# Two-layer attention and state-space block on one core: loads reordered, key weights' halves in further buffers, gate taken by halves of its PSUM pair

## What is computed

```python
for l in range(2):
    sh, sc, gt = split(silu(c) @ w_ada[l] + b_ada[l])          # the same with c_ctx for the context
    h  = rms_norm(x, norm_pre[l]) * (1 + sc) + sh
    hc = rms_norm(ctx, norm_pre[l]) * (1 + scc) + shc
    if l == 0:  # qa, ka, va, ga, qb, kb, vb, gb = split(h @ w_in); two kinds of attention, 16 heads, 4 key groups
        y, yc = attn_mixer(...)                                 # softmax attention, times silu(gate), @ w_out
    else:       # z, xbc, dt = split(h @ w_in); conv, silu; a chunked two-way state-space scan in 8 groups
        y = gated_rms_norm(scan + D * x, z, norm_w) @ w_out     # y * silu(z), normed by group
    x = x + gt * rms_norm(y, norm_post[l])
```

## Time and profile before

| what | value |
|---|---|
| median of 3 runs | 1668.16 us (1666.35 to 1669.1) |
| the profiled execution, own time | 1661.65 us |
| its span (first to last instruction) | 1659.9 us |
| PE busy | 1449.7 us, 87% of the span |
| PEld busy | 1270.8 us, 77% |
| DVE busy | 994.7 us, 60% |
| ACT busy | 703.4 us, 42% |
| POOL busy | 303.2 us, 18% |
| mean granted PE clock | 0.942 of full speed |
| transfers | 124.41 MB, 75 GB/s over the span |

### The profile page before, as it was taken

How to read it: one execution, slowest core, us unless ns; L and a number is a source line. 1 busy time by engine, 2 the same in 40 slices (tenths; PEclk the granted TensorE clock), 3 DMA queues, 4 the chain that set the end, 5 groups by cost and what they waited for, 6 DMA issues and landing times.

```text
span 1659.9 us, 23265 instructions
## 1 busy us (share of the span) xinstructions
PE 1449.7 (87%) x8440; PEld 1270.8 (77%) x8440; DVE 994.7 (60%) x1782; ACT 703.4 (42%) x1456; POOL 303.2 (18%) x294
## 2 busy tenths in 40 slices
PE   5789899999989889869995899899898989897797
PEld 5678787888778788758874787888788887886575
DVE  5575666667657676644206566767676767666322
ACT  5221344434334433323216455555545555555331
POOL 0000000000000000002223241414233231413143
PEclk9999899999999999979997999999999999996799
DMA  9243111211112111124411111111101111110431
GB/s 357 72 144 127 39 49 57 87 47 47 57 38 88 54 48 48 48 95 146 158 45 63 54 52 39 63 38 51 62 28 62 38 63 38 57 70 0 171 134 64
DMA packets 37957, 124.41 MB, mean 75 GB/s; under 512 B 5392, under 2 KB 5648, under 8 KB 37904
## 3 DMA queue, kind: packets, MB, share of 16 engines
q1 hardware_dynamic: 33296, 113.21, 19.5%
q10 hardware_dynamic: 4608, 10.49, 2.0%
HBM read 109.00 MB, written 14.68 MB: 75 GB/s over the span
## 4 chain that ended last, share of the span: by engine, by line
PE 50%; DVE 17%; issue 13%; ACT 9%; POOL 8%; DMA 3%; SPq 0%; DVEq 0%; ACTq 0%; POOLq 0%
PE psL L1763 12%; PE psL L2062 4%; PE psC L1763 4%; POOL xw L1726 3%; PE psS L1748 3%; PE psS L1750 3%; PE psS L1749 3%; PE psV L1748 3%; PE psV L1750 2%; PE psV L1749 2%; POOL Hlo L1732 2%; PE psL L1748 2%; DVE smax L1216 2%; PE psL L1750 2%; DVE PTlo L1255 2%
## 5 line engine op out<-in xcount | busy, mean ns | idle before, releaser
L1763 PE MATMUL psL<-hhi,whi 128*128 128x512 f32 x320 | 132.7, 415 | 0.0
L1763 PE MATMUL psL<-hlo,whi 128*128 128x512 f32 x320 | 131.5, 411 | 0.0
L1763 PE MATMUL psL<-hhi,wlo 128*128 128x512 f32 x320 | 130.6, 408 | 0.0
L1611 POOL TENSOR_TENSOR rq<-vq,half 128x6 f32<-128x6 f32 x10 | 16.1, 1606 | 601.3 <-DVE vq L1109 601.3
L1615 POOL TENSOR_TENSOR wlo<-wraw,whi 128x1024 fp32r<-128x1024 f32 x34 | 81.6, 2399 | 236.2 <-ACT whi L570 140.1
L1748 PE MATMUL psV<-PThi,Vhi 128*128 128x256 f32 (+1 forms) x224 | 71.5, 319 | 38.2 <-DVE PTlo L1255 27.6
L1763 PE MATMUL psC<-hhi,whi 128*128 128x256 f32 x296 | 88.9, 300 | 17.4 <-DVE wlo L1075 7.4
L2062 PE MATMUL psL<-h1hi,whi 128*128 128x512 f32 x256 | 103.2, 403 | 0.0
L2062 PE MATMUL psL<-h1hi,wlo 128*128 128x512 f32 x256 | 101.6, 397 | 0.0
L2062 PE MATMUL psL<-h1lo,whi 128*128 128x512 f32 x256 | 101.4, 396 | 0.0
L1255 DVE TENSOR_TENSOR PTlo<-psT,PThi 128x256 fp32r<-128x256 f32 (+3 forms) x96 | 67.9, 707 | 42.1 <-ACT PThi L711 41.9
(11 more groups left out here) (399 smaller groups left out, 4722.9 us busy)
## 6 DMA issues: line engine op xcount, KB each, us to landing
wraw<-in_w_ssm SPq DMA_DIRECT2D x48, 512.0 KB, 3.2
wraw<-in_w_in SPq DMA_DIRECT2D x40, 512.0 KB, 4.5
wraw<-in_w_out SPq DMA_DIRECT2D x32, 512.0 KB, 4.0
ada<-in_w_ada SPq DMA_DIRECT2D x16, 512.0 KB, 15.1
wraw<-in_w_ada_late SPq DMA_DIRECT2D x16, 512.0 KB, 5.3
X<-in_xc SPq DMA_DIRECT2D x12, 512.0 KB, 8.7
y_spill<-Yst SPq DMA_DIRECT2D x16, 384.0 KB, 2.6
X<-y_spill ACTq DMA_DIRECT2D x16, 384.0 KB, 3.2
```

Source lines behind the costliest of these rows:

```text
L1763: last = PE_.matmul(out, a, b, start=i == 0 and not shared, stop=i == 3 * KT - 1, skip_group_check=True)
```

## The change

It has four edits, three on the first 175 us and one in the state-space groups. Edits without an effect on any order (names of semaphores, three signals instead of two for a group's z) are left out of the diff.

1. SP issues `early_load(0)` to `(2)`, three token tiles, `early_load(3)`, the other three token tiles, then `early_load(4)` and on. The three tables `costab`, `sintab`, `rowt` are loaded right behind the third tile of `w_in`, before the wait for `s_h_lo`; their buffers and `PThi`, `PTlo` move to the end of the allocation, and `junk0` is gone: the tanh of `crow` lies in the last two `ada` tiles until they are loaded (`early_load(7)` now waits for its use), the reductions' unused products in free parts of `hhi` and `hlo`.
2. Kind 0 of odd tiles 1 and 3 has its halves in `PThi` and `PTlo`, buffers of the attention that are free in this stage. So the halves of kind 0 are made one tile earlier: w = 2 within tile 0's stage, w = 2g+4 in group g behind `gate_tile(4g)`. `made(w)` gives the count that w has in the new order. SP's waits for raw buffers follow it.
3. `key_hi` and `key_lo` of groups 0 and 1 come ahead of `Vhi` and `Vlo`, with semaphores of their own (`s_key_hi`, `s_key_lo`). `q_hi(4)` and `q_lo(4)` come right behind the first head's evacuation and rope.
4. In the state-space groups z's second half-product is made for blocks 2 and 3 first, then 0 and 1; tanh and `sz` are made in two instructions of 512 columns, the second bank first. `cb(0)` waits for the first of these, the steps for the second. `gsel` is copied ahead of `GP`, with one semaphore for both.

```diff
     with ExitStack() as s:
...
-        junk0 = sbuf(s, "junk0", [P, 2, D_MODEL])
+    tanh_rows = ada[:, ADA_EARLY - 2:ADA_EARLY].rearrange("p n a b -> p n (a b)")
+    sum_junk = [h[:].rearrange("p k t -> p (k t)")[:, 6 * TOK:6 * TOK + D_MODEL] for h in (hhi, hlo)]
...
+    def made(w):
+
+        if 3 <= w < W_HEAD0 + 1:
+            return w + 2 if w % 2 else w
+        return w + 1
+
+    def weight_buffers(e, kind):
+
+        if kind == 0 and isinstance(e, int) and e < GROUPS and e % 2:
+            return tuple(b[:].rearrange("p t q -> p (t q)")[:, 0:D_MODEL].rearrange("p (a b) -> p a b", a=KT) for b in (PThi, PTlo))
+        return whi[:, kind], wlo[:, kind]
...
-        early_load(0)
-        early_load(1)
-        for t in range(TT):
+        def x_load(t):
+
             sp.dma_start(X0[:, t, :], io["xc"][t]).then_inc(s_x_loaded[t // 2], 16)
 
+        for k in range(3):
+            early_load(k)
+        for t in range(TT // 2):
+            x_load(t)
+        early_load(3)
+        for t in range(TT // 2, TT):
+            x_load(t)
+
...
-        for k in range(2, KT):
+        for k in range(4, KT):
+            if k == KT - 1:
+                sp.wait_ge(s_silu_rows, 2)
             early_load(k)
             if k == KT - 3:
                 w_in_load(0)
                 w_in_load(1)
         w_in_load(2)
-        w_in_load(3)
-        for u in range(NR, NR + 2):
-            sp.wait_ge(s_weight_lo, u - 3)
-            w_in_load(u)
-        sp.wait_ge(s_h_lo, KT)
         sp.dma_start(costab[:], io["cos"]).then_inc(s_tables_loaded, 16)
         sp.dma_start(sintab[:], io["sin"]).then_inc(s_tables_loaded, 16)
         sp.dma_start(rowt[:], io["rows"][ROWS["sink"][0]:ROWS["sink"][1]].partition_broadcast(P)).then_inc(s_tables_loaded, 16)
+        w_in_load(3)
+        for u in range(NR, NR + 2):
+            sp.wait_ge(s_weight_lo, made(u - NR))
+            w_in_load(u)
+        sp.wait_ge(s_h_lo, KT)
...
         h_scaled(0)
         h_scaled(1)
+        weight_hi(1, 0, 2, 1)
...
             q_lat(g, norm, scale)
-            weight_hi(g + 1, 0, (2 * g + 2) % NR, (2 * g + 2) // NR + 1)
+            if g + 2 <= GROUPS:
+                weight_hi(g + 2, 0, (2 * g + 4) % NR, (2 * g + 4) // NR + 1)
...
+            if g < 2:
+                key_hi(g)
             act.wait_ge(s_v_transposed, g + 1)
...
-            if g < 2:
-                key_hi(g)
         q_ctx(GROUPS, False, 1.0)
         q_lat(GROUPS, False, 1.0)
+        q_hi(GROUPS, 0)
         gate_ctx(GROUPS)
         gate_lat(GROUPS)
         key_hi(3)
-        q_hi(GROUPS, 0)
...
-            act.wait_ge(s_z_weight_used, 2 * g + 2)
-            A_.activation(thz[:], psS[:, :], ACT.Tanh, scale=0.5).then_inc(s_z_tanh, 1)
+            for n in range(2):
+                x = slice(512 * (1 - n), 512 * (2 - n))
+                act.wait_ge(s_z_weight_used, 3 * g + 2 + n)
+                A_.activation(thz[:, x], psS[:, x], ACT.Tanh, scale=0.5).then_inc(s_z_tanh, 1)
...
         for k in range(2, KT):
             h_split(k)
+            if k == 3:
+                weight_lo(2, 0, 2)
...
             rope(g)
-            weight_lo(2 * g + 2, 0, (2 * g + 2) % NR)
             gate_tile(4 * g)
+            if g + 2 <= GROUPS:
+                weight_lo(2 * g + 4, 0, (2 * g + 4) % NR)
             gate_tile(4 * g + 1)
...
         rope(GROUPS)
+        q_lo(GROUPS, 0)
         key_normed(3)
         gate(GROUPS, 0, 0)
         gate(GROUPS, 0, 1)
         key_lo(3)
-        q_lo(GROUPS, 0)
...
-            dve.wait_ge(s_z_tanh, g + 1)
-            V_.scalar_tensor_tensor(sz, thz[:], 1.0, psS[:, :], ALU.add, ALU.mult).then_inc(s_z_silu, 1)
+            for n in range(2):
+                x = slice(512 * (1 - n), 512 * (2 - n))
+                dve.wait_ge(s_z_tanh, 2 * g + n + 1)
+                V_.scalar_tensor_tensor(sz[:, x], thz[:, x], 1.0, psS[:, x], ALU.add, ALU.mult).then_inc(s_z_silu, 1)
...
-            z(1, (0, 1))
             z(1, (2, 3)).then_inc(s_z_weight_used, 1)
+            z(1, (0, 1)).then_inc(s_z_weight_used, 1)
             log_decays(0)
-            pe.wait_ge(s_z_silu, g + 1)
+            pe.wait_ge(s_z_silu, 2 * g + 1)
             pe.wait_ge(s_bc_lo, g + 1)
             cb(0)
+            pe.wait_ge(s_z_silu, 2 * g + 2)
```

More of the change, by code:

```diff
@@ L151, in build @@
         junkm = sbuf(s, "junkm", [P, 1, D_MODEL])
+        PThi = sbuf(s, "PThi", [P, TT, 2 * P], f32r)
+        PTlo = sbuf(s, "PTlo", [P, TT, 2 * P], f32r)
+        rowt = sbuf(s, "rowt", [P, 8])
+        nsink = sbuf(s, "nsink", [P, 8])
+        costab = sbuf(s, "costab", [P, SEQ])
+        sintab = sbuf(s, "sintab", [P, SEQ])
     ph.close()
@@ L252, in build @@
     s_rope_step = sem("rope_step")
-    s_q_hi, s_q_lo = sem("q_hi"), sem("q_lo")
+    s_q_hi, s_q_lo, s_key_hi, s_key_lo = sem("q_hi"), sem("q_lo"), sem("key_hi"), sem("key_lo")
     s_qk_square_sums, s_qk_variance, s_qk_rstd = sem("qk_square_sums"), sem("qk_variance"), sem("qk_rstd")
@@ L568, in weight_hi @@
             act.wait_ge(s_raw_weights_loaded[slot], 16 * use)
-            free_hi_lo(act, w, par, tile)
-            A_.activation(whi[:, par], wraw[:, slot], ACT.Copy).then_inc(s_weight_hi, 1)
+            if par == 0 and isinstance(tile, int) and 0 < tile <= GROUPS:
+                if tile > 1:
+                    act.wait_ge(s_q_lat_proj, tile - 1)
+            else:
+                free_hi_lo(act, w, par, tile)
+            A_.activation(weight_buffers(tile, par)[0], wraw[:, slot], ACT.Copy).then_inc(s_weight_hi, 1)
         act.wait_ge(s_small_loaded, 64)
         A_.activation(cth[:], csilu[:], ACT.Tanh, scale=0.5).then_inc(s_silu_c_step, 1)
-        A_.activation(junk0[:], crow[:], ACT.Tanh, scale=0.5).then_inc(s_silu_rows, 1)
+        A_.activation(tanh_rows, crow[:], ACT.Tanh, scale=0.5).then_inc(s_silu_rows, 1)
         for t in range(TT):
@@ L1072, in weight_lo @@
         def weight_lo(w, par, slot):
-            dve.wait_ge(s_weight_hi, w + 1)
-            V_.tensor_tensor(wlo[:, par], wraw[:, slot], f(whi[:, par]), ALU.subtract).then_inc(s_weight_lo, 1)
+            dve.wait_ge(s_weight_hi, made(w) if isinstance(w, int) else w + 1)
+            hi, lo = weight_buffers(w // 2 if isinstance(w, int) else w, par)
+            V_.tensor_tensor(lo, wraw[:, slot], f(hi), ALU.subtract).then_inc(s_weight_lo, 1)
         early_sums(0)
@@ L1155, in _ @@
                 key_lo(2)
+            if g < 2:
+                key_lo(g)
             if g >= 2:
@@ L1165, in _ @@
                 last.then_inc(s_k_rstd_diag, 1)
-            else:
-                key_lo(g)
             gate_tile(4 * g + 2)
@@ L1760, in project @@
                 k, m = divmod(i, 3)
-                a = (whi, whi, wlo)[m][:, par, k, :]
+                hi, lo = weight_buffers(e, kind)
+                a = (hi, hi, lo)[m][:, k, :]
                 b = (hhi, hlo, hhi)[m][:, k, toks]
```

59 lines of the change are left out of this document (27 added, 32 removed).

## The result

| | kernel before | changed kernel |
|---|---|---|
| median | 1668.63 us (4 runs, 1666.35 to 1672.08) | 1641.81 us (4 runs, 1639.39 to 1644.03) |
| profiled execution, own time | 1661.65 us | 1644.03 us |
| its span | 1659.9 us | 1642.3 us |
| PE, DVE, ACT, POOL busy | 1449.7, 994.7, 703.4, 303.2 us | 1445.0, 995.0, 704.0, 303.0 us |

The changed kernel is faster, by 1.6%: ratio 0.9837, 95% interval 0.9815 to 0.9859. The medians lie 26.8 us apart, the two profiled executions 17.6. Forecast were 1648.8 us and a difference of 19.4.

The account below looks back on a forecast made before the run. PE, busy 87% of the span, was taken as the bound, through standing still or lower clock. Terms -18.7 - 0.85 + 2.3 - 2.2 = -19.4 us, from median 1668.16 to 1648.8 us; range 1638 to 1657.

Parts of the forecast that it names:

- Edit 2, 18.7 us: Key and value stage: shorter waits and no slow tails at tiles 1 to 3, 7.62 + 5.08 + 5.98 us gained.
- All three gaps: PE's waits at kind 0 of three tiles in the key stage: 7.4, 3.33 and 6.7 us, plus slow matmuls behind.
- the margin at kind 1: Key stage: kind 1's low half ready at 83.7, wanted at 84.0; 0.3 us spare in group 0, 0.5 in group 1.
- Edit 3, 0.85: Before attention: one 0.95 us subtraction leaves DVE's stretch before `reduce_max`; gain 0.85 us, bounds 0 and 3.8.
- Edit 1, a loss of 2.3: First loads: last tokens land at 26.04 instead of 20.92, PE's first transposes move to 37.25; loss 2.3 us, bounds 0 and 5.1.
- Edit 4, "0.27 us a group, 2.2 for eight": State-space groups: `cb(0)` hides under the gate's second half, first step comes 0.27 us earlier; 2.2 us for eight, low bound 0.
- The clock rival: State-space groups: the shorter gap of some 2.3 us avoids the clock's fall; 14 us more, hence 1635; chance 0.12.
- Waits added, 0: Added waits in each group and for each attention head lie next to waits ending later; 0, bounds 0 and 1 us.
- The second wait: State-space groups: a short further wait of PE, after the wait of about 2.3 us on the silu.
- the forecast's own 1644 to 1654: Whole kernel: range in us of the main forecast without rivals, chance 0.63; with rivals 1638 to 1657.

Follow-up runs that it names:

- the trace with filling in its groups: Kernel before with 16 matmuls, their result overwritten, added where PE stood idle in seven state-space groups; 1658.70 us, ratio 0.9954.

## Why the prediction was right, and where it was off

**Edit 2, 18.7 us: right in place and nearly in size.** All three gaps went, bank `psC` was late next, the margin at kind 1 held (0.66 us where 0.3 was put). Up to tile 1 the sum said -6.13 + 2.3 = -3.83 and the traces show 77.49 - 80.92 = -3.43. From tile 1 to the norm it said 12.55; the traces show 89.81 - 78.70 = 11.1. The missing 1.4 is the row at 144.70: I took it that a gap of 1.3 us has nearly no slow tail, from a single row. Of the ten traces with the changed key stage eight have it at 4.4 to 4.6 us, with the granted clock falling at that row, and two at 3.08. The three traces with the old key stage have 3.06 to 3.09. So a gap of 1.3 us can have a tail; what decides is not settled. The tails of the old form are not fixed either: 4.34, 4.60 and 5.46 us in the trace before, 5.46 in all three of the trace with filling in its groups, which is most of why the norm is 14.5 us apart in one pair of traces and 17.6 in another. The forecast for edits 1 and 2, 16.4, lies between.

**Edit 3, 0.85: right,** 0.79 measured. **Edit 1, a loss of 2.3: right,** 2.3 to 2.9 measured; the 2.56 us per MB of the earlier trace rows carried it. The tokens' squares came at 26.38, where transfers in order put them at 26.04, so what the Trainium skill (DMA: Bandwidth & Descriptors, Queues, rings and completion order) says of transfers that complete out of order did not bear here. That this edit is a loss the experiment with the old order confirms in the trace; its median alone would not.

**Edit 4, "0.27 us a group, 2.2 for eight": this is the term that was mis-sized.** As a shortened path it was well put: the wait is 2.30 us as forecast, the first step comes 0.25 us earlier (0.27 forecast), and the edit is worth 0.18 a group once the clock is out of it. The Trainium skill (VectorE: DVE Perf Modes, The TRN2 errata) led to an estimate of 0.18 too, but by a cost of 0.16 for the split; the rows show 0.06, 1.27 against 1.21, so the agreement is not the page's. The mistake was to price the gap without what follows it, though edit 2 was priced with its tails. Over seven groups the edit is worth 7.1 us against the same kernel with the old gate, 4.2 against the kernel before (521.67 - 517.43), where the forecast has 1.9.

The clock rival asked whether the clock stays up behind the shorter gap (14 us). In the changed kernel it does not: it falls in all seven groups, for 3.4 us in six and nearly 7 in one. The price was also wrong. The clock kept up in all seven groups is worth 6.3 us to the kernel before, not 14: the group of 73.86 us, taken as still losing one stretch, loses nothing, as a group takes 73.83 to 73.86 with the clock up; PE then waits about 1 us for the update of the state instead. The rival drew on the Trainium skill (TensorE: Matmul & The Clock Gate, Part 1), by which a shorter gap is caught less often. The traces bear this out in part. Of 14 gaps of 2.83 us (the kernel before and the changed one with the old gate) none escapes and 11 have the long stretch; of 56 gaps of 2.30 us, in the eight traces with the halves and without filling, 2 escape and 13 have it.

The traces say more on the length. In all these 70 groups the stretch is the long one where the clock had fallen 0.27 us or more before PE went on (24 groups), and in the other 46 it is 3.4 us or there is none; there the clock fell 0.20 us before or later, or not at all. With the old gate it had fallen 0.55 us before in the group shown (1038.35 against 1038.90), and a group with the long stretch takes 75.13 to 75.19 us, while its falls follow each other at 75.09: the next gap meets the fall at nearly the same place, and the long stretch repeats. The kernel before is caught late three times, then early in the fourth group, and stays so for all that follow; the changed kernel with the old gate is caught early from the first on. With the halves such a group takes 74.65, the next gap comes 0.4 us earlier against the fall, and after one or two groups the long stretch ends. That is what the halves bought from the clock. Where the first group meets the fall differs from one execution to another.

**Waits added, 0: right within what can be seen.** The second wait that the forecast had shows as 0.4 us from the last matmul of `cb(0)` to the first step, instead of 0.12; no other new wait of PE stands in the groups.

**The sum against the two measures.** From the traces: 14.5 up to the norm, 0.8 in front of attention, 4.2 in seven groups, 19.5 us. That this equals the 19.4 forecast is in part luck: up to the norm the forecast has 16.4 and the traces 1.9 less, in seven groups it has 1.9 and the traces 2.3 more. The profiled executions differ by 17.6: from norm to first gate the changed kernel gained another 1.9 us, and from the last gate to the end it took 165.6 us against 161.7. Its second trace took 161.6, and all traces together 161.6 to 167.0, so that is scatter and not the change. The medians differ by 26.8 and, when repeated, 25.7 (23 by the ratio). So 1641.81 lies 7 us under the forecast, within the stated range of 1638 to 1657 but outside the forecast's own 1644 to 1654. The profiled execution of the kernel before was 7.0 us under its median, that of the changed one 2.2 over. The prediction carried the difference of one execution over to the median. What the usual execution of the kernel before loses in addition is not in any trace here. It may have the long stretch in more groups: its clock was 0.942 in the trace, and the 34 executions run beside the last eight experiments go from 0.935 to 0.947, the quickest, 1653.73 us, at 0.945 and the slowest, 1670.69, at 0.935. Against it stands that the gate halves alone brought the kernel before 3 us by the ratio, 6 at the end of its interval, where seven long stretches would be worth 524.65 - 517.03 = 7.6. The cause stays open.

## What to carry to other kernels

A gap of PE costs its length and the time at 1.2 GHz behind it; price both in every term, also where an edit only shortens a gap that stays. To find out how much hangs on the clock, fill the gap with matmuls that nobody reads and compare both versions filled: that took 7.1 us down to 1.3. Where a gap recurs, look at when the clock falls against PE's next matmul, and whether the period repeats that place. And compare small edits at fixed places of two traces, as 0.8 us between two DVE rows was plain where medians could not tell 3.

## What the runs showed that was not expected

The narrow matmuls of the prologue run at two speeds while the windows show a granted clock of 1.00. One line's instructions, in the repetition of the changed kernel (duration min/median/max in ns):

```profile
L1874 PEld LDWEIGHTS psL<-csilu,ada x64: 192/333/337, 17.7 to 41.7; 128*128 128x128 f32 x64
```

and in its first trace:

```profile
L1874 PEld LDWEIGHTS psL<-csilu,ada x16: 333/333/337, 40.0 to 43.2; 128*128 128x128 f32 x16
```

A weight load of these matmuls takes 192 ns at 2.4 GHz and 333 at 1.2: in the repetition they go from 192 to 333 where the recorded clock falls to 0.50, at 43.6 us. The 16 matmuls from 40 us took 1.92 us in one and 3.41 in the other, and the first projection started at 47.98 and at 51.13. So before the first change that the profile records the clock column can't be trusted; the duration of a weight load can. What decides it was not tried.

The stretch from norm to first gate, which of all edits only edit 3 touches, by 0.8 us at its start, took 799.5 to 807.9 us in the traces. That is the widest scatter of any stretch read here; how much of the differences between medians it makes is not shown, with one trace for each kernel and two for the changed one.
